# A two-layer decoder trunk on one core: the start's order, products of constants in two waits, the convolution's tap schedule, and the totals' engine

## The reference

```python
h = rmsnorm(x, w['norm1_g'])
(q_m, k_m, v_m, i_pre, f_pre, o_pre, glu_a, glu_b, q_a, k_a, v_a, g_pre) = split_cols(h @ w['w_in'])
hm = mlstm(q_m, k_m, v_m, i_pre, f_pre, state)                  # chunks of 16, 128, 128; c_new, n_new, m_new
y_a = (sigmoid(o_pre) * hm) @ w['w_mlstm_out']
u = glu_a * sigmoid(glu_b)
uc = depthwise_conv(u, state_conv, w['w_dconv'], b_dconv)       # 31 taps, 512 channels
y_b = silu(layernorm(uc, ln_conv_g, ln_conv_b)) @ w['w_conv_out']
oa = sink_attention(rope(q_a), rope(k_a), v_a)                  # window 128, 8 heads, 2 KV heads
y_c = oa @ w['w_attn_out']
x = x + (g_a * y_a + g_b * y_b + g_c * y_c) @ w['w_out']
x = x + (silu(conv3(h2 @ w_ffn_gate)) * (h2 @ w_ffn_up)) @ w['w_ffn_down']     # h2 = rmsnorm(x)
```

## Time and profile before

| | us |
|---|---|
| median of 3 runs | 1043.05 (1042.21 to 1044.66) |
| profiled execution | 1041.96 |
| span of its trace, first to last instruction | 1039.8 |
| PE busy | 1004.8 |
| DVE busy | 770.2 |
| ACT busy | 571.8 |
| POOL busy | 39.9 |

### The profile page before, as it was taken

How to read it: one execution, slowest core, us unless ns; L and a number is a source line. 1 busy time by engine, 2 the same in 40 slices (tenths; PEclk the granted TensorE clock), 3 DMA queues, 4 the chain that set the end, 5 groups by cost and what they waited for, 6 DMA issues and landing times.

```text
span 1039.8 us, 19576 instructions
## 1 busy us (share of the span) xinstructions
PE 1004.8 (97%) x7896; PEld 959.4 (92%) x7896; DVE 770.2 (74%) x1475; ACT 571.8 (55%) x1079; POOL 39.9 (4%) x55
## 2 busy tenths in 40 slices
PE   4999999999999999999979999999999999999997
PEld 3999989988999999999979998898899999999997
DVE  4577897876787877775574879978678877887563
ACT  4545665646646655553344465657466655665542
POOL 0011000021000000000000200000210000000000
PEclk9999999999999999999989999999999999999998
DMA  9754546456545765555487546363755667666552
GB/s 237 179 146 128 128 116 163 124 140 173 159 138 163 233 199 168 170 165 172 148 194 162 147 128 143 104 180 103 184 167 165 166 165 243 182 183 178 171 171 76
DMA packets 318659, 167.92 MB, mean 161 GB/s; under 512 B 25294, under 2 KB 317502, under 8 KB 318506
## 3 DMA queue, kind: packets, MB, share of 16 engines
q1 hardware_dynamic: 318426, 165.87, 58.3%
q10 hardware_dynamic: 144, 0.80, 0.2%
HBM read 160.11 MB, written 9.71 MB: 163 GB/s over the span
## 4 chain that ended last, share of the span: by engine, by line
PE 83%; DVE 6%; ACT 5%; DMA 3%; issue 2%; SPq 0%; DVEq 0%
PE ps_tile L949 17%; PE ps_tile L950 16%; PE ps_tile L951 16%; PE work L949 7%; PE work L951 7%; PE work L950 7%; DMA w_raw<-in_w_in 2%; DVE w_lo L1883 2%; ACT w_hi L1359 1%; ACT scores L1515 1%; PE work L1183 1%; PE work L1185 1%; PE work L1193 1%; PE work L1167 1%; DVE prod L1940 1%
## 5 line engine op out<-in xcount | busy, mean ns | idle before, releaser
L1883 DVE TENSOR_TENSOR w_lo<-w_raw,w_hi 128x1024 fp32r<-128x1024 f32 (+1 forms) x288 | 343.1, 1197 | 99.5 <-ACT w_hi L1359 98.6
L1359 ACT ACTIVATE w_hi<-w_raw 128x1024 fp32r<-128x1024 f32 (+1 forms) x288 | 295.3, 1028 | 148.6 <-DMA w_raw<-in_w_in 65.9
L949 PE MATMUL ps_tile<-h_hi,w_hi 128*128 128x280 f32 (+2 forms) x944 | 282.8, 300 | 9.1 <-DVE h_lo L1893 8.9
L950 PE MATMUL ps_tile<-h_lo,w_hi 128*128 128x280 f32 (+2 forms) x944 | 275.7, 292 | 0.0
L951 PE MATMUL ps_tile<-h_hi,w_lo 128*128 128x280 f32 (+2 forms) x944 | 275.3, 292 | 0.0
L949 PEld LDWEIGHTS ps_tile<-h_hi,w_hi 128*128 128x128 f32 (+1 forms) x944 | 178.4, 189 | 15.3 <-issue 13.0
L950 PEld LDWEIGHTS ps_tile<-h_lo,w_hi 128*128 128x128 f32 (+1 forms) x944 | 178.4, 189 | 1.1
L951 PEld LDWEIGHTS ps_tile<-h_hi,w_lo 128*128 128x128 f32 (+1 forms) x944 | 178.0, 189 | 0.6
L949 PE MATMUL ps_tile<-xg_hi,w_hi 128*128 128x280 f32 (+2 forms) x368 | 106.4, 289 | 0.3 <-DVE w_lo L1883 0.3
L951 PE MATMUL ps_tile<-xg_hi,w_lo 128*128 128x280 f32 (+2 forms) x368 | 105.8, 287 | 0.0
L950 PE MATMUL ps_tile<-xg_lo,w_hi 128*128 128x280 f32 (+2 forms) x368 | 105.8, 287 | 0.0
(11 more groups left out here) (377 smaller groups left out, 1822.3 us busy)
## 6 DMA issues: line engine op xcount, KB each, us to landing
w_raw<-in_w_in SPq DMA_DIRECT2D x98, 512.0 KB, 3.9
w_raw<-in_w_ffn_gate SPq DMA_DIRECT2D x44, 512.0 KB, 3.9
w_raw<-in_w_ffn_up SPq DMA_DIRECT2D x44, 512.0 KB, 3.9
w_raw<-in_w_ffn_down SPq DMA_DIRECT2D x32, 512.0 KB, 3.6
w_raw<-in_w_out SPq DMA_DIRECT2D x16, 512.0 KB, 3.7
w_raw<-in_w_ffn_down SPq DMA_DIRECT2D x14, 384.0 KB, 3.2
w_raw<-in_w_in SPq DMA_DIRECT2D x20, 256.0 KB, 3.6
c_head<-in_state_mlstm_c SPq DMA_DIRECT2D x8, 512.0 KB, 5.6
```

Of the source, the lines that this page charges most:

```text
L949: mm(out, hi[:, k, :], a_hi[:, k0 + k, f:T], start=first, stop=False, skip_group_check=True)
L950: mm(out, hi[:, k, :], a_lo[:, k0 + k, f:T], start=False, stop=False, skip_group_check=True)
L1359: go(h, r, ACT.Copy).then_inc(w_hi_ready, 1)
L1883: tt(lo, r, h.bitcast(F32), ALU.subtract).then_inc(w_split[n % SLOTS], 1)
```

## The change

1. Start: PE first waits for the copy of the identity in fp32r (`mask_r`, ACT L1346), turns all of x, and only then spreads the inverse roots. Behind that it makes 14 products of constants, 128 columns wide, into a bank that nobody reads before it is written anew. ACT splits piece 1 ahead of `rms_inv`; DVE takes `split_lo(0)` after `invert_rows`, `split_lo(1)` after the copies, and `split_lo(2)` after the first `h_lo`.
2. Between the layers PE makes 14 products of constants, 432 columns wide, after `turn_norm`.
3. Taps begin at n = 5, a chunk's once its glu_a piece is done. There are 2, 3, 3, 5, 5 at n = 5 to 9 (before 0, 0, 0, 4, 4), 3 at n = 10 (before 2), 6 at n = 11 to 13 (before 4), 2 at even n from 22 to 36 (before 4), and the rest is as before.
4. `block_att_lo` goes ahead of `softmax_unit_2` on DVE.
5. Both totals go from POOL to DVE: that of the squares ahead of `add_outer` at n = 51, the other after it at n = 49.

```diff
-CONV_FROM, CONV_TO = 8, 49
-BUSY = {10: 2, 14: 0, 15: 0, 16: 3, 17: 1, 18: 1, 19: 0, 20: 1, 37: 5, 38: 5, 39: 0, 40: 3, 41: 1, 42: 5,
+CONV_FROM, CONV_TO = 5, 49
+BUSY = {5: 2, 6: 3, 7: 3, 8: 5, 9: 5, 10: 3, 11: 6, 12: 6, 13: 6, **{n: 2 for n in range(22, 37, 2)}, 14: 0, 15: 0, 16: 3, 17: 1, 18: 1, 19: 0, 20: 1, 37: 5, 38: 5, 39: 0, 40: 3, 41: 1, 42: 5,
         **{n: 6 for n in range(43, 49)}, **{n: 2 for n in range(21, 37, 2)}}
+def tap_order():
+    order, done = [], [0] * KC
+    for n, count in enumerate(TAPS_AT):
+        for _ in range(count):
+            open_chunks = [c for c in range(KC) if STEP["glua", c] < n and done[c] < CONV_W]
+            if open_chunks:
+                c = min(open_chunks, key=lambda c: (done[c], c))
+                order.append((n, done[c], c))
+                done[c] += 1
+    return order
...
+            def keep_running(bank, source, count):
+                for _ in range(count):
+                    mm(bank[:, 0:source.shape[1]], mask_r[:, 0:P], source, start=True, stop=True)
...
+            pe.wait_ge(masks_ready, 1)
             for i, k in enumerate((2, 3)):
                 pe.wait_ge(x_in[i], 16 * k)
             for c in range(KD):
...
-                if c == 7:
-                    for b, (t0, n) in enumerate(ROW_BLOCKS):
-                        pe.wait_ge(diagonal_ready, b + 1)
-                        mm(work[4][:, t0:t0 + n], ones[0:n, 0:P], row_inverse[0:n, b, 0:n], start=True, stop=True)\
-                            .then_inc(inv_rows_spread, 1)
...
+            for b, (t0, n) in enumerate(ROW_BLOCKS):
+                pe.wait_ge(diagonal_ready, b + 1)
+                mm(work[4][:, t0:t0 + n], ones[0:n, 0:P], row_inverse[0:n, b, 0:n], start=True, stop=True)\
+                    .then_inc(inv_rows_spread, 1)
+            keep_running(ps_tile[1], mask_r[:, 0:P], 14)
...
                 if l > 0:
                     turn_norm(l, work[1], 0)
+                    keep_running(work[4], mask_r[:, P:P + SOURCE_COLS], 14)
...
                     take_norm(ps_tile[2][:, 0:KD])
+                    split_hi(1)
                     act.wait_ge(inv_rows_spread, 3)
                     go(rms_inv[:, :], work[4][:, 0:T], ACT.Copy).then_inc(rms_inv_ready, 1)
-                    split_hi(1)
                     split_hi(2)
...
-                    if n == 49:
-                        total_conv()
-                    if n == 51:
-                        total_conv_squares()
...
                 if c == 4:
                     invert_rows()
+                    split_lo(0, 0)
+            split_lo(1, 0)
...
-                        if l == 0 and c < 2:
-                            split_lo(c + 1)
                         if c >= 1:
                             lo(c - 1)
+                        if l == 0 and c == 1:
+                            split_lo(2, 0)
...
+                    if n - 1 in VALUES_AT[1::2]:
+                        block_att_lo(VALUES_AT.index(n - 1) // 2)
                     if n - 2 in SCORES_AT:
                         softmax_unit_2(SCORES_AT.index(n - 2))
                     if n == 22:
                         sample_att_lo()
-                    if n - 1 in VALUES_AT[1::2]:
-                        block_att_lo(VALUES_AT.index(n - 1) // 2)
...
+                    if n == 51:
+                        total_conv_squares()
                     if n in OUTER_AT:
                         add_outer(OUTER_AT.index(n))
+                    if n == 49:
+                        total_conv()
```

More of the change, by code:

```diff
@@ L227 @@
 assert sum(TAPS_AT) >= KC * CONV_W
+def tap_order():
[7 more added lines that the diff above has]
+                done[c] += 1
+    assert len(order) == KC * CONV_W
+    return order
+TAPS = tap_order()
+TAP_NO = {(tap, c): i for i, (_, tap, c) in enumerate(TAPS)}
 SCORES_AT = [21 + 2 * u for u in range(6)]
@@ L1763, in _ @@
             for l in range(DEPTH):
[L1764 to L1779, removed]
                 def rope_cosine():
@@ L1845, in invert_rows, with split_lo @@
                     ts(row_inverse[0:n, b, 0:n], ident[0:n, 0:n], row_invs[0:n, b:b + 1], None, ALU.mult).then_inc(diagonal_ready, 1)
+            def split_lo(n, l):
+                dve.wait_ge(w_hi_ready, value("w_hi_ready", l, n + 1))
+                r, h, lo = split_views(n, 0, PIECES[n][2])
+                tt(lo, r, h.bitcast(F32), ALU.subtract).then_inc(w_split[n % SLOTS], 1)
             for c in range(KD):
@@ L1978, in take, with taps @@
                         tt(merged[:, t, f:T], old, prod[:, t % 2, f:T], ALU.add).then_inc(merged_ready, 1)
-                def taps(first, count):
-                    for i in range(first, min(first + count, KC * CONV_W)):
-                        tap, c = divmod(i, KC)
-                        w, dst, src = vcol("w_dconv", i), uc[:, c, 0:NP], u_pad[:, c, tap:tap + NP]
+                def taps(n):
+                    for at, tap, c in TAPS:
+                        if at != n:
+                            continue
+                        w, dst, src = vcol("w_dconv", tap * KC + c), uc[:, c, 0:NP], u_pad[:, c, tap:tap + NP]
                         if tap == 0:
-                            if c == 0:
-                                dve.wait_ge(took_dve, value("took_dve", l, DVE_NO["glua", KC - 1] + 1))
-                                dve.wait_ge(pad_zero, value("pad_zero", l, 1))
-                                dve.wait_ge(vec_ready, value("vec_ready", l, 2))
+                            dve.wait_ge(took_dve, value("took_dve", l, DVE_NO["glua", c] + 1))
+                            dve.wait_ge(pad_zero, value("pad_zero", l, 1))
+                            dve.wait_ge(vec_ready, value("vec_ready", l, 2))
                             ts(dst, src, w, vcol("b_dconv", c), ALU.mult, ALU.add).then_inc(tap_done, 1)
                         else:
-                            dve.wait_ge(tap_done, value("tap_done", l, i - KC + 1))
+                            dve.wait_ge(tap_done, value("tap_done", l, TAP_NO[tap - 1, c] + 1))
                             stt(dst, src, w, dst, ALU.mult, ALU.add).then_inc(tap_done, 1)
@@ L2202, in centre, with total, total_conv, total_conv_squares @@
                         stt(uc[:, c, :], work[0][:, 0:T], -1.0 / C_CONV, uc[:, c, :], ALU.mult, ALU.add).then_inc(centred, 1)
+                def total(src, k):
+                    dst = conv_total[:, k, :]
+                    tt(dst, src[:, 0, :], src[:, 1, :], ALU.add).then_inc(conv_added, 1)
+                    for c in (2, 3):
+                        dve.wait_ge(conv_added, value("conv_added", l, 3 * k + c - 1))
+                        tt(dst, dst, src[:, c, :], ALU.add).then_inc(conv_added, 1)
+                def total_conv():
+                    dve.wait_ge(tap_done, value("tap_done", l, KC * CONV_W))
+                    dve.wait_ge(hist_sum, value("hist_sum", l, 5))
+                    total(uc, 0)
+                def total_conv_squares():
+                    dve.wait_ge(ln_sq, value("ln_sq", l, 1))
+                    total(conv_sq, 1)
                 def norm_conv():
@@ L2245, in act_los @@
                         tt(act_lo[:, t, f:T], gate_buf[:, t % 4, f:T], act_hi[:, t, f:T].bitcast(F32), ALU.subtract).then_inc(act_lo_ready, 1)
-                if l == 0:
-                    split_lo(0)
                 first_norm()
-                split_lo(3)
+                split_lo(3, l)
                 nc.vector.memset(u_pad[:, :, 0:HIST], 0.0).then_inc(pad_zero, 1)
@@ L2258, in _ @@
                     for i in splits_first(n):
-                        split_lo(i)
+                        split_lo(i, l)
                     for tile in PIECES[n][4]:
@@ L2267, in _ @@
                     if splits_later(n):
-                        split_lo(n + AHEAD)
+                        split_lo(n + AHEAD, l)
                     elif l + 1 < DEPTH and N_PIECES - AHEAD <= n < N_PIECES - 1:
@@ L2317, in _ @@
                         decayed_scores(ML_AT.index(n))
-                    taps(sum(TAPS_AT[:n]), TAPS_AT[n])
+                    taps(n)
             last = D_MODEL - P
```

4 lines of the change are left out of this document (removed).

## The result

The changed kernel takes 1054.84 us in the median of 4 runs (1051.97 to 1059.17), the kernel before 1042.63 of 4 (1041.26 to 1044.66). The ratio is 1.0116, with a 95% interval of 1.0096 to 1.0135. I had forecast 1040.0 with a range up to 1044.2: wrong in sign. The profiled execution took 1051.97, with a span of 1049.8, 10.0 above the span before. It is the fastest of the four: what follows accounts for these 10 us, and the traces of the slower three were not kept.

A forecast was written before the change was run, and what follows sets the result against it. PE, busy 97% of the span, was taken to bound the kernel. Gains of 8.2 us less losses of 5.1 gave 3.1 less, 1038.9 for the profiled execution and a forecast median of 1040.0, range 1036.0 to 1044.2.

The forecast's parts named there:

- Start, order: At the start, the new order brings the first product at about 19.6 instead of 22.52: 2.9 us gained.
- Start, constants: At the start, 14 constants at 0.11 us each stay hidden in the wait and speed the first products: 0.5 us gained.
- The first rival: Start constants raise the clock at once and POOL's head start softens the rope: 1036.9 us, chance 0.20.
- Between the layers: 14 constants at 0.20 us each fit PE's wait and keep the clock up for layer 2's first products: 2.6 us gained.
- Attention: At n = 30, att_lo ahead of the softmax shortens PE's wait, with a new wait behind it: 2.2 us over two layers.
- Taps: Seven more taps ahead of the rope, 0.41 us each, make PE wait at turn_kv beyond the slack: 3.7 us lost.
- the lower end: Taps at the rope: POOL's cosines get ahead, one no longer in DVE's way in each layer: 1.1 us lost.
- the upper end: Taps at the rope: they hold POOL up as well, so the slack is used up without them: 5.8 us lost.
- Totals: At c_head, three additions on DVE cost 1.3 us, partly offset by a faster w_lo: 0.68 per layer, 1.4 lost.
- The slower one: Constants at the start, perhaps also between the layers, cost more than their place holds: 1046.3 or 1049.0 us, chance 0.10.
- The range: Whole kernel: 1036.0 to 1044.2 us, taking in the forecast and two rivals, leaving out the dear constants.

The follow-up runs named there:

- e9: The changed kernel with ten early taps and ten fewer at n = 10 to 13, squares' total behind c_head, no start constants: 1031.61 us, ratio 0.9903.
- e10: e9 without the constants between the layers too, so no product of constants at all: 1032.91 us, ratio 0.9921 to the kernel before.
- e2: The changed kernel with POOL's cosines waiting until the taps of n = 13 are done: 1045.68 us, ratio 1.0045 to the kernel before.
- e4: The changed kernel with 20 products of constants, 432 columns wide, on PE ahead of the rope's product: 1049.43 us, ratio 1.0070 to the kernel before.
- e5: The kernel before with only the start's order and constants, the constants between the layers and att_lo's place changed: 1038.33 us, ratio 0.9958.
- e8: e5 with both totals on DVE, that of the squares behind the update of c_head: 1037.12 us, ratio 0.9928 to the kernel before.
- e6: e5 without any product of constants, at the start or between the layers: 1037.64 us, ratio 0.9938 to the kernel before.
- e7: e5 with ten early taps at n = 5 to 9, taken from n = 10 to 13: 1036.97 us, ratio 0.9931 to the kernel before.

## Why the prediction was wrong, step by step

**Start, order: right.** 2.9 forecast; `h_lo` ends at 19.0 instead of 22.4, in an execution in which x came 0.5 earlier (the first turn at 7.90 instead of 8.37): 2.9. **Start, constants: wrong in price and in gift.** I took 0.11 each and a gain of 0.5; they cost 0.22 each at the slow pace, outlasted `h_lo` by 0.8, and the kernels without them show no loss. The point from which they begin to cost, 0.16 each, was in the text. The first rival, constants that speed up the first products at once, did not come either: 9 to 22 of these were slow.

**Between the layers: right.** 0.20 each, as forecast, a step of 2.8 against 2.6 (25 steps of 0.11 would be 2.7). e9 and e10 put it at 1.3 in the median.

**Attention: right** in layer 1, 1.2 against 1.1, with the new wait at the next step. Layer 2 gained 1.6, by luck: the text took its wait to be layer 1's 1.64, but it was 2.4, and 0.8 of it is left.

**Taps: this step failed.** The sum took seven taps at 0.41 us, a price read from taps that had DVE's neighbour idle, and put what POOL's cosines do to a tap at nothing. Cosines stood in it only as something that gets out of DVE's way (the lower end) or is held up itself (the upper end, 2.9 a layer). The row of 75.14 showed the cosines starting as the taps ended; putting more taps there meant putting them beside the cosines. Its 5.20 for four also hid that the first cosine alone took 2.54, beside the last taps and a `w_lo`, and the others 0.8 to 1.0; the text read 1.3 on the mean. Six taps then cost 5.20, and e2 gives 2.6 back by holding POOL alone.

The place was wrong as well. PE waited not at `turn_kv` but at the product before it, which needs the first sine. In the kernel before, DVE had 2.0 us in hand there in layer 1 and 1.5 in layer 2, with 0.14 taken off for the hand-over (in the changed kernel the sine ends at 81.18 and PE starts at 81.32). And the slack was read from the kernel before, although the start's gain moves PE more than DVE: PE came to the rope of layer 1 3.0 us earlier, DVE only 2.2, as its `w_lo` of piece 14 waits for data (60.71 instead of 62.87). So the wait of 4.4 in layer 1 adds up: 2.9 for seven taps, 2.7 for five slow ones, 0.8 for PE's lead, less 2.0 in hand. In layer 2 it is 2.9 and 2.7 less 1.5. With POOL held back, in e2, PE's waits at both ropes come to 4.3, near the sum's 3.7: the seven taps themselves were priced about right, in part by luck, as the slack and the place were not.

The second half of the failure is the clock: for a new wait of PE I priced the wait and no more, though the first wait of 3.71 had shown what follows one. The waits of 4.4 and 4.0 were followed by a low clock (0.70 in layer 1), 1.6 us more in each layer, and e4 gives 1.5 back in layer 2. In layer 1 it does not: there the clock falls a little later in e4, as it does in e5 to e8, of which e6 and e7 have no wait there. So of the 11.6 us at the two ropes I had 3.7; 8.5 are waits and 3.1 the slow stretches behind them.

**Totals: the sign right, the size not.** The relief of `w_lo` came as forecast. The three additions took 1.9 instead of 1.3, beside POOL's next work, which I had not moved forward in my head when I took the totals off its queue: PE lost 1.3 a layer instead of 0.7. And the same omission of the clock: 3.0 us behind the wait of layer 2. That part is chance as far as the runs show, since behind the eight such waits on record the clock fell twice.

**The rivals.** The slower one that I gave was dear constants, at 0.10. What happened, a collision of taps and cosines with a fall of the clock behind the wait, was not among the rivals, though both halves were in the text: the lock of the shared port, quoted for `w_lo`, holds for the taps by the same words, since a tap reads SBUF twice. The Trainium skill, "SBUF — State Buffer", SBUF: two separate sides, says that of a DVE operation with two SBUF inputs and a POOL operation whichever starts first has the pair for its whole instruction; the rows of one tap and one cosine in each 0.95 us agree with that.

**The range.** It went wrong at its upper end because taps were priced without a neighbour and new waits of PE at their length. The Trainium skill, "TensorE: Matmul & The Clock Gate", HAM oscillation — how this bites in real kernels, says that a wait between groups of products can let the clock fall back and that each time the return is paid anew; e4 agrees in the window behind the wait, 0.70 with the wait open and 1.00 with it filled; the low clock of e7, behind products and no wait, is not of this kind.

## What to carry to other kernels

Before an instruction is moved to another place in a queue, look at what the neighbouring engine does at that time, not only at what stands in the same queue. Here DVE's taps and POOL's cosines, which both read SBUF twice, took turns, and a gain elsewhere was enough to bring them together (e5); leaving the stretch free cured it (e7). Read the slack for the moved times, not for the old ones: a gain that brings one engine forward by 3.0 us and the other by 2.2 uses up slack. A new wait of TensorE may cost more than its length: the added 1.3 us cost 1.3 in six places of eight here and 4.3 to 4.4 in two. The constants were worth their place in the one wait that was longer than they were (between the layers); where they outlasted the wait (the start) they cost.

## What the runs showed that I had not expected

A product of 128 columns cost 0.22 us at the slow pace, nearly as much as one of 280 columns (0.23), while one of 432 cost 0.20 at the full pace.

The same kernel, in two layers with nearly the same wait, can keep the clock in one and lose it in the other, and in another execution of a kernel that differs elsewhere the other way round (changed kernel and e4, n = 53). The executions of some kernels lie several us apart: 7.2 us over 4 runs of the changed kernel, 2.1 over 5 of e9. Long waits alone don't explain it: e8, in which PE waits at most 0.9 at the rope and not at all for `c_head`, has 5.4 over 4.

POOL's first cosine lasted 2.7 us while DVE made taps and a `w_lo` without a break, and 2.5 in the kernel before; each later one of these two lasted 0.8 to 1.0. Once the first was over, taps and cosines alternated one by one. It is not always so: in e5 the first cosine of layer 1 began amid taps, too, and took 0.85. What makes the first one long is open.
